# The state space chunks in wide matmuls, their halves added by VectorE

## The reference, cut to what matters

```python
proj = h @ w_in                                    # h: 256 x 2048
xbc = silu(causal_depthwise_conv(xbc, conv_w, conv_b))
xs, Bm, Cm = split(xbc)
dt = softplus(dt_raw + dt_bias);  A = -exp(a_log)
y = ssd_chunked(xs, dt, A, Bm, Cm)                 # two chunks of 128 tokens, state passed on
y = y + d_skip * xs
y = y * silu(z)                                    # the gate
y = y * rsqrt(mean(y * y, over a group) + EPS) * ssm_norm_w
merged = sigmoid(g_attn) * (attn @ w_attn_proj) + sigmoid(g_ssm) * (y @ w_ssm_proj)
```

## Time and profile before

| | |
|---|---|
| median of three runs | 3328.04 us (3322.73 to 3331.66) |
| profiled execution | 3328.01 us, span 3326.2 us |
| TensorE busy | 3227.2 us, 97% |
| VectorE busy | 2254.3 us, 68% |
| ScalarE busy | 1547.1 us, 47% |
| mean granted TensorE clock | 0.992 |
| chain that ended last | 86% on TensorE, 6% VectorE, 3% DMA, 2% ScalarE |
| HBM traffic | 208 GB/s over the span |
| first four state space groups | 434 to 702 us |
| last four | 795 to 1066 us |

### The profile page before, as it was taken

The page is one execution under the profiler, slowest core; times in us unless marked ns, Lnnn a source line. Parts: engine busy times, 40 slices in busy tenths (PEclk is TensorE's granted clock), DMA queues, the critical chain, the costliest instruction groups (busy, mean ns, idle before and its releaser), DMA issues.

```text
span 3326.2 us, 53885 instructions
## 1 busy us (share of the span) xinstructions
PE 3227.2 (97%) x22929; PEld 2988.1 (90%) x22929; DVE 2254.3 (68%) x2733; ACT 1547.1 (47%) x1603; POOL 0.2 (0%) x4
## 2 busy tenths in 40 slices
PE   6999999999999999999999999999999999999999
PEld 4888999989999799988888888889899999999987
DVE  5787567778777878777776565776555654555676
ACT  2333666634555344433333333466656474443333
POOL 0000000000000000000000000000000000000000
PEclk9999999999999999999999999999999999999999
DMA  9887554556454776566665566545533444455554
GB/s 376 337 313 257 187 182 181 179 235 253 178 180 177 301 261 247 189 248 232 228 230 202 183 204 202 185 165 177 207 129 139 164 168 149 152 179 209 208 184 158
DMA packets 110419, 693.12 MB, mean 208 GB/s; under 512 B 11519, under 2 KB 18751, under 8 KB 36324
## 3 DMA queue, kind: packets, MB, share of 16 engines
q1 hardware_dynamic: 97776, 655.30, 54.0%
q10 hardware_dynamic: 12404, 34.38, 2.8%
HBM read 679.05 MB, written 13.72 MB: 208 GB/s over the span
## 4 chain that ended last, share of the span: by engine, by line
PE 86%; DVE 6%; DMA 3%; ACT 2%; DVEq 1%; issue 1%; ACTq 0%; SPq 0%
PE accp L507 22%; PE accp L512 14%; PE accp L514 14%; PE accp L513 14%; PE accp L508 12%; DVE wlo L1611 2%; DMA raw<-w 2%; PE accp L510 1%; ACT whi L1087 1%; PE pw L588 1%; DVE macc L1674 1%; PE pw L993 1%; PE pw L1028 1%; PE pw L578 1%; DVE macp L1674 1%
## 5 line engine op out<-in xcount | busy, mean ns | idle before, releaser
L1611 DVE TENSOR_TENSOR wlo<-raw,whi 128x2048 fp32r<-128x2048 f32 (+1 forms) x544 | 1201.8, 2210 | 553.8 <-ACT whi L1087 548.4
L1087 ACT ACTIVATE whi<-raw 128x2048 fp32r<-128x2048 f32 (+1 forms) x544 | 1002.9, 1847 | 612.5 <-DMA raw<-w 579.9
L512 PE MATMUL accp<-act,whi 128*128 128x256 f32 x3680 | 1063.3, 289 | 14.3 <-ACT gl L1097 5.4
L514 PE MATMUL accp<-act,wlo 128*128 128x256 f32 x3680 | 1044.0, 284 | 0.0
L513 PE MATMUL accp<-act,whi 128*128 128x256 f32 x3680 | 1043.9, 284 | 0.0
L512 PEld LDWEIGHTS accp<-act,whi 128*128 128x128 f32 x3680 | 708.8, 193 | 24.7 <-issue 9.5
L513 PEld LDWEIGHTS accp<-act,whi 128*128 128x128 f32 x3680 | 708.9, 193 | 5.4 <-issue 5.0
L514 PEld LDWEIGHTS accp<-act,wlo 128*128 128x128 f32 x3680 | 708.5, 193 | 0.0
L507 PE MATMUL accp<-act,whi 128*128 128x512 f32 x1830 | 650.8, 398 | 1.5 <-DVE tf L1621 0.9
L508 PE MATMUL accp<-act,wlo 128*128 128x256 f32 x1952 | 527.8, 281 | 0.0
L507 PEld LDWEIGHTS accp<-act,whi 128*128 128x128 f32 x1830 | 343.7, 188 | 80.7 <-DVE tf L2138 1.2
(11 more groups left out here) (503 smaller groups left out, 4165.1 us busy)
## 6 DMA issues: line engine op xcount, KB each, us to landing
raw<-w SPq DMA_DIRECT2D x480, 1024.0 KB, 4.8
raw<-w SPq DMA_DIRECT2D x64, 704.0 KB, 4.1
mraw_a<-wm SPq DMA_DIRECT2D x38, 1024.0 KB, 8.3
mraw_b<-wm SPq DMA_DIRECT2D x24, 1024.0 KB, 8.9
mraw_c<-wm SPq DMA_DIRECT2D x16, 1024.0 KB, 6.9
mraw_x<-wm SPq DMA_DIRECT2D x10, 1024.0 KB, 14.8
acb<-ac_d ACTq DMA_DIRECT2D x8, 1024.0 KB, 4.7
mraw_w<-wm SPq DMA_DIRECT2D x8, 1024.0 KB, 7.0
```

Of the source, the lines that this page charges most:

```text
L512: pe.matmul(acc[:, 0:S], wh, x2[:, 0, :], start=first, stop=False)
L514: mm = pe.matmul(acc[:, 0:S], wl, x2[:, 0, :], start=False, stop=last)
L1087: act.activation(whi[:, c % 4, 0:k, :], raw[:, c % 4, 0:k, :], ACT.Copy).then_inc(hi_done, 1)
L1611: dve.tensor_tensor(wlo[:, c % 4, 0:k, :], raw[:, c % 4, 0:k, :], whi[:, c % 4, 0:k, :].bitcast(F32), ALU.subtract).then_inc(lo_done, 1)
```

## The change

All 80 state space results become wide, so TensorE issues two matmuls per k instead of three, and all 80 are moved by VectorE, which adds the halves. For j < 6 the sum goes to `ub`, directly ahead of its convolution. For j >= 6 it goes to `sz`, as the last thing of VectorE's step j, and ScalarE then applies Silu on `sz` in place (`shape`), waiting for that sum; before it gates y, VectorE waits for the fourth of these (`shaped`). ScalarE's 48 moves to `ub` and its wait for `grp` are gone.

```diff
-        for name, n in (("fi", 44), ("pg", 16)):
+        for name, n in (("ssm0", 16), ("ssm1", 16), ("fi", 44), ("pg", 16)):
...
-                by_dve = lead or name in SUMS or name[:2] == "br" and i % 4 >= 2
+                conv = name[:3] == "ssm"
+                by_dve = lead or conv or name in SUMS or name[:2] == "br" and i % 4 >= 2
...
-                WIDE.append(name in SUMS and not triple and not lead)
+                WIDE.append(conv or name in SUMS and not triple and not lead)
...
@@ ScalarE, group @@
                     if j < 6:
-                        act.wait_ge(conv_d, 6 * g + 1 + j)
-                        take(c, e, ub[:, j % 2, 3:259])
                         if j == 0 and g % 4:
                             act.wait_ge(ssq_v, g)
                             act.activation(rstd[:, :], st0[:, 0:S], ACT.Sqrt).then_inc(ssq_r, 1)
                     else:
-                        if j == 6:
-                            act.wait_ge(grp, g + 1)
-                        take(c, e, sz[:, j - 6, :], ACT.Silu)
+                        shape(e, sz[:, j - 6, :], ACT.Silu)
...
@@ VectorE, group @@
                 def convolve(j):

-                    dve.wait_ge(*out_of((E0[ph] + 10 * gg + j + 20 * i) + 1))
+                    add(C0[ph] + 10 * gg + j + 20 * i, E0[ph] + 10 * gg + j + 20 * i, ub[:, j % 2, 3:259])
+                    dve.drain()
                     dve.wait_ge(silu_d, 6 * g + j + 1)
...
+                    if j >= 6:
+                        add(C0[ph] + 10 * gg + j + 20 * i, E0[ph] + 10 * gg + j + 20 * i, sz[:, j - 6, :])
-                dve.wait_ge(*out_of((E0[ph] + 10 * gg + 9 + 20 * i) + 1))
+                dve.wait_ge(shaped, SH0["ssm0"] + 4 * g + 4)
```

More of the change, by code:

```diff
@@ L1252, in _, with shape @@
             act.wait_ge(ac_st, 16)
+            def shape(e, buf, func, **kw):
+                act.wait_ge(*out_of(e + 1))
+                act.activation(buf, buf, func, **kw).then_inc(shaped, 1)
             def group(i, h, gg):
@@ L1302, in group @@
                     act.activation(rstd[:, :], st0[:, 0:S], ACT.Sqrt).then_inc(ssq_r, 1)
-            def shape(e, buf, func, **kw):
-                act.wait_ge(*out_of(e + 1))
-                act.activation(buf, buf, func, **kw).then_inc(shaped, 1)
             for h in range(2):
```

## The result

The changed kernel takes 3387.36 us in the median of four runs (3382.62 to 3392.07), the kernel before 3328.47 (3322.73 to 3331.66): 1.0181 times as long, 95% interval 1.0168 to 1.0193. Forecast were 3377, in a range of 3348 to 3400.

What follows compares the result with a forecast made beforehand. TensorE, busy 97% of the span, was taken to bound the kernel, with 0.3 us margin at xdd. Six groups x (4.8 + 2.5) = 43.8 plus two x (2.0 + 0.8) = 5.6 made +49.4 on 3328.0: 3377 us, range 3348 to 3400.

Steps and rivals of the forecast that it cites:

- The place and the ring: Before xdd at chunk 8's end: VectorE and ScalarE take turns (sum, silu, whi, wlo, xdt), 5.5 us a turn.
- A regular group: Each of six groups (all but first and fifth): +4.8 us net, plus 2.5 us for the fallen clock.
- stall: TensorE stands after chunk 8 until VectorE's xdd is done at 620.5 instead of 615.2: 5.5 us.
- bank of chunk 6: TensorE's chunk 8 waits 0.3 us for the bank that the sum of chunk 6 frees.
- narrower stream, ten chunks: TensorE's wide chunks take 5.65 us instead of 5.75: 0.10 us saved a chunk, 1.0 a group.
- clock: After TensorE stands 5.5 us, granted clock is 0.50 for 5.6 us in the mean: 2.5 us lost each time.
- The upper bound of this term, +15 us: Allowance around the clock's 16.6 us in all, if the clock falls longest.
- Groups 1 and 5: The two lighter groups, each half's first: TensorE stands about 3.0 us, net +2.0 plus 0.8 for the clock, 5.6 together.
- the clock holds through the stall (3361): Rival 1: VectorE and ScalarE take turns, but the clock holds through 5.5 us: 3361 us; chance 0.10.
- the sums hide (3322): Rival 2: sum of chunk 6 on time, VectorE's spare time covers all 80 sums: 3322 us; chance 0.08.
- Rival 3: Sums delay the convolutions, thus decay's silu and ramps on ScalarE; VectorE 2 us later a group: 3393 us; chance 0.12.

Runs made afterwards that it cites:

- the filled stall: Changed kernel plus 12 matmuls of unread result a group (11 in the first, 7 in the fifth) ahead of TensorE's wait for xdd: 3361.44 us.
- both reorderings: Changed kernel with xdd made ahead of the subtraction (wlo) of chunk 10 and each silu one step later, behind whi: 3327.36 us, ratio 0.9988.
- the three reorderings: Changed kernel with xdd ahead of chunk 10's wlo, silu a step later, and chunk 6's sum ahead of chunk 8's wlo: 3322.96 us, ratio 0.9989.

## Why the prediction was right

**The place and the ring: right.** The xdd matmul as the only large wait; releaser VectorE; once a group; silu, whi, wlo and sum taking turns. Forecast were 5.5 us a turn, measured 630.13 to 635.65, 5.52. The sum of chunk 6 was to be 5.7 us behind TensorE; the transposes behind that chunk begin at 623.81 in TensorE's timeline, and the sum at 630.13: 6.3. The stall was to be 5.5 and is 5.3. Undoing one link of the ring (the silu later), or taking xdd out from behind it, removes it, and the sums stay. That makes the cause shown, not argued.

**A regular group: +7.3 forecast, +7.13 measured.** Its terms:

| term | forecast | measured | from |
|---|---|---|---|
| stall | 5.5 | 5.3 | waits of after |
| bank of chunk 6 | 0.3 | 0.65 | waits of after |
| narrower stream, ten chunks | -1.0 | -1.0 to -1.2 | three kernels without the stall |
| clock | 2.5 | 1.98 | the filled stall |
| sum | 7.3 | 6.7 to 6.9, whole group 7.13 | |

The stream: with only the convolution's results wide, (64.81 - 64.19) / 6 = 0.10 us a chunk; with both reorderings (64.81 - 64.27 + 0.7) / 10 = 0.12; with the sum first as well (64.81 - 63.99 + 0.42) / 10 = 0.12. Some 0.2 to 0.4 us a group has no row that I can name. That the whole is nearer than its terms is in part luck: the clock was 0.5 us too high, the bank 0.35 and the part without a row 0.2 to 0.4 too low.

**The clock: the term was there, a fifth too large.** The forecast took 5.6 us at 0.50, the mean of what followed the ends of six gaps of 3.3 to 4.0 us in the kernel before, and carried it over to a stall of 5.5. But behind the longer stall less of the low stretch is left: the clock is down already in the window 640 to 642, when nothing runs and nothing is lost by it. From 642.08 to shortly after 646 are some 4.2 us of work at the low level, which is also the mean behind the six stalls, and half of that is 2.1, beside the 1.98 of the filled stall; by the forecast's own 0.45 it would be 1.9. The Trainium skill (TensorE: Matmul & The Clock Gate, HAM oscillation — how this bites in real kernels) works such a loss out as the throttled time x (1 - 1.2 / 2.4). Put to the 5.6 us that the forecast took, that rule gives 2.8, too much; put to the 4.2 us in which the array works it gives 2.1, and the trace agrees with its 1.98.

The upper bound of this term, +15 us, did not follow from the 3.3 us that the forecast allowed a stall at most: 6 x (3.3 - 2.5) + 2 x (3.3 - 0.8) = 9.8. The measured time lies inside with either.

**Groups 1 and 5: the step that was under-sized.** Forecast +2.8 each, 5.6 together; measured +7.1 (from the value product to the first y matmul, 67.8 instead of 60.7) and +4.2 (172.95 instead of 168.73 from the fourth y to the fifth), 11.3 together. The forecast walked through VectorE's queue in the fifth group alone and took the first to be like it. The stall of the fifth is 3.16 us, as forecast (3.0); that of the first is 4.9. The first group of the program starts late, on ScalarE and then on VectorE, and VectorE has no slack to make it good:

```profile
445.04 3.72 ACT L1088 ACTIVATE whi<-raw 128x2048 fp32r<-128x2048 f32 x2 [6.46 <-DMA gs_d<-gsb]
```

```profile
446.99 2.29 DVE L1608 TENSOR_TENSOR wlo<-raw,whi 128x2048 fp32r<-128x2048 f32 x1 [5.86 <-ACT whi L1088]
449.20 0.68 DVE L1618 TENSOR_REDUCE ub<-accp 128x256 f32<-128x512 f32 x1
```

The start is as late in the kernel before (6.00 us of idle time ahead of ScalarE's whi at 437.04); what is new is the work behind it. From 446.99 to the sum of chunk 6 at 486.31 VectorE stands 2.4 us in all, and never for a result of TensorE. In the fifth group it still waits for one three times (1.30, 0.48 and 0.56 us), so it is on time there. The kernel without the six sums of the convolution bears this out: its stalls are 3.12 us in the first group and 2.66 in the fifth. No run took the late start itself away.

And the second half of that step, 0.8 us of clock for a stall of about 3, was too little: the filled kernel is 1.8 us shorter than the changed one in the first group and 2.7 in the fifth. In the fifth group the clock fell before the stall was over at 886.31:

```profile
884.00:886.00 2.00, 0.00 (x0) 0.80 0.81 238
886.00:888.00 2.00, 1.69 (x3) 0.50 0.70 291
888.00:890.00 2.00, 2.00 (x7) 0.50 0.00 0
...
892.00:894.00 2.00, 2.00 (x13) 0.99 0.04 8
```

**The sum.** Six groups 42.8 where 43.8 were forecast, groups 1 and 5 11.3 where 5.6 were: 54.1 us against 49.4. The second comparison of the same two kernels has 3383.11 - 3328.32 = 54.8, so the groups are all of it. The first comparison has 58.9, and its profiled execution 64.1, of which 7.5 lie ahead of the first group (439.3 against 431.8). The 4 us between the two comparisons are the repeat's own difference.

**The rivals.** That the clock holds through the stall (3361) is refuted; the kernel in which it does hold, by force, takes 3361.44. That this is the rival's number is chance: its groups cost 37.8 us where the rival had 32.8, and the rest lies outside them. That the sums hide (3322) is refuted for this order and true for another: 3322.96 with the three reorderings. Rival 3, VectorE later still, happened in the first group alone, and by the late start rather than by the ramps that it named: VectorE waits 1.98 us there for a whi behind the ramps, but 3.23 us at the same ramps in the kernel before. VectorE's idle time is enough for 80 sums; it was the order that didn't let them in.

**What stays open.** With xdd ahead, the median is 9.0 us above the kernel before and the groups explain 2.5; with the stall filled, the median is 32 above and the groups explain 37.8. So some microseconds lie outside the groups, of either sign. The profiled executions show where. With xdd ahead, 5.6 of 8.9 us lie ahead of the first group (last value product at 437.4 instead of 431.8); filled, the time behind the last group's first y matmul is 2269.8 us instead of 2276.1 (2274 in the kernel before's repeat). Ahead of the first group the time goes with the granted clock of that stretch. A window of it, after and then before:

```profile
300.00:350.00 50.00, 44.74 (x292) 0.90 0.56 197
```

```profile
300.00:350.00 50.00, 45.73 (x328) 0.97 0.66 217
```

Over 60 to 430 us, the mean granted clock is 0.99 in the four profiles whose last value product is at 431.8 to 432.6, 0.98 in the four with 433.6 to 435.4, and 0.97 in the three with 437.4 to 439.3. The two programs that were profiled twice have two of these values each, so it is at least in part a matter of the execution and not of the program. Whether the clock makes this stretch longer or idle times there make both is not shown, and for the microseconds behind the last group I have no cause.

## What to carry to other kernels

When work moves from one in-order engine to another, add up not the engine's free time but the ring: follow each new wait through what is queued behind the waiting instruction until the path returns to its start, and compare one round with the consumer's period. If the round is near it, put the new dependent step behind the instruction that the other engine waits for, or take the consumer's input out from behind it; either here gave back nearly all of 54 us. And walk the first round of a loop on its own: what feeds it is seldom what feeds the rest.

## What was unexpected in the hardware

A gap of 3.16 us in the fifth group cost the clock as much of a stretch at 0.50 as those of 5.3, and more of it fell into work (5.7 us against 4.2); it was taken for a borderline case. With only the gate's results wide, the gap of 3.12 us in the first group was followed by 0.50 too, that of 2.66 in the fifth was not.

VectorE's rows have short idle times that nothing in the profile explains. Two of after, the second in the fourth group:

```profile
451.97 0.48 DVE L1912 SCALAR_TENSOR_TENSOR cv<-ub,cst,cv 128x256 f32<-128x256 f32 x1 [0.43 <-issue]
```

```profile
713.53 0.69 DVE L1955 TENSOR_TENSOR xdd<-xdt,decn 128x512 f32<-128x512 f32 x1 [0.46 <-issue]
```

They come at few places (four in the eight groups of after), and need not cost anything: the first is followed by a wait of 1.98 us for ScalarE at 464.42, which takes it up. The second did cost something: it stands directly ahead of xdd, and its group's stall is 5.66 us where the other five have 5.29 or 5.30. The repeat has 0.44 and 5.65 at the same place.
